# Attention scores in a hybrid encoder block: queries and keys kept as a high and a low part, heads taken one after the other

## The reference

```
for i in range(S // Q_BLOCK):                      # 4 query blocks of 128
    lo, hi = i * Q_BLOCK, (i + 1) * Q_BLOCK
    s = einsum('bhqd,bhkd->bhqk', qh[:, :, lo:hi], kh[:, :, :hi]) * scale
    s = s + cum_f[:, :, lo:hi, None] - cum_f[:, :, None, :hi]
    p = softmax(where(causal, s, -inf), axis=-1)
    outs.append(einsum('bhqk,bhkd->bhqd', p, vh[:, :, :hi]))
```

## Time and profile before

| | |
|---|---|
| median of three runs | 1771.42 us (1770.65 to 1771.48) |
| the profiled execution | 1769.05 us, span 1767.5 us |
| PE busy | 1723.1 us (97%) |
| DVE busy | 1343.8 us (76%) |
| ACT busy | 1108.6 us (63%) |
| attention steps q = 0 to 15 | from 260.6 us on, to the last transposes at 398.8 us |

### The profile page before, as it was taken

The page is one execution under the profiler, slowest core; times in us unless marked ns, Lnnn a source line. Parts: engine busy times, 40 slices in busy tenths (PEclk is TensorE's granted clock), DMA queues, the critical chain, the costliest instruction groups (busy, mean ns, idle before and its releaser), DMA issues.

```text
span 1767.5 us, 23399 instructions
## 1 busy us (share of the span) xinstructions
PE 1723.1 (97%) x8257; PEld 1403.7 (79%) x8258; DVE 1343.8 (76%) x1175; ACT 1108.6 (63%) x935; POOL 283.6 (16%) x227
## 2 busy tenths in 40 slices
PE   6999999999999999999999999999999999999995
PEld 5777788888887777888878888888888888888884
DVE  6334323442446898999999999999999999999998
ACT  3534434473322467777777777777777777777775
POOL 3000000000001162221212122212121212122211
PEclk9999999999999999999999999999999999999998
DMA  7432231212242599999999999999999999999994
GB/s 263 121 96 72 72 96 48 72 49 96 95 143 84 196 344 396 363 374 381 388 376 373 370 383 372 369 373 387 373 372 377 387 364 372 387 387 360 369 381 164
DMA packets 115696, 487.98 MB, mean 276 GB/s; under 512 B 18911, under 2 KB 49631, under 8 KB 66496
## 3 DMA queue, kind: packets, MB, share of 16 engines
q1 hardware_dynamic: 99576, 455.76, 67.0%
q0 software_dynamic: 16064, 31.55, 6.4%
q10 hardware_dynamic: 8, 0.01, 0.0%
HBM read 476.22 MB, written 28.36 MB: 285 GB/s over the span
## 4 chain that ended last, share of the span: by engine, by line
PE 90%; DVE 4%; ACT 2%; issue 2%; DMA 2%; ACTq 0%; POOLq 0%; DVEq 0%; SPq 0%
PE psA L1635 21%; PE psA L1637 21%; PE psA L1636 21%; PE psX L1637 6%; PE psX L1635 6%; PE psX L1636 6%; PE psX L1642 3%; DVE wlo L1382 2%; DMA raw<-in_w_down 1%; PE psX L1816 1%; ACT whi L961 1%; PE psX L1802 1%; PE psA L2011 1%; PE psX L1825 0%; PE psA L1891 0%
## 5 line engine op out<-in xcount | busy, mean ns | idle before, releaser
L1382 DVE TENSOR_TENSOR wlo<-raw,whi 128x2048 fp32r<-128x2048 f32 x382 | 863.2, 2287 | 63.7 <-ACT whi L961 62.5
L961 ACT CAST whi<-raw 128x2048 fp32r<-128x2048 f32 x382 | 724.7, 1913 | 199.6 <-PE psA L1637 170.1
L1635 PE MATMUL psA<-whi,xT_hi 128*128 128x512 f32 x1036 | 407.4, 393 | 2.2 <-issue 2.2
L1637 PE MATMUL psA<-whi,xT_lo 128*128 128x512 f32 x1036 | 404.0, 390 | 0.0
L1636 PE MATMUL psA<-wlo,xT_hi 128*128 128x512 f32 x1036 | 403.9, 390 | 0.0
L1635 PEld LDWEIGHTS psA<-whi,xT_hi 128*128 128x128 f32 x1036 | 195.0, 188 | 43.5 <-issue 4.2
L1637 PEld LDWEIGHTS psA<-whi,xT_lo 128*128 128x128 f32 x1036 | 194.8, 188 | 40.9
L1636 PEld LDWEIGHTS psA<-wlo,xT_hi 128*128 128x128 f32 x1036 | 194.9, 188 | 39.2
L1635 PE MATMUL psX<-whi,aT_hi 128*128 128x512 f32 x496 | 195.8, 395 | 0.0
L1637 PE MATMUL psX<-whi,aT_lo 128*128 128x512 f32 x496 | 193.4, 390 | 0.0
L1636 PE MATMUL psX<-wlo,aT_hi 128*128 128x512 f32 x496 | 193.3, 390 | 0.0
(11 more groups left out here) (371 smaller groups left out, 1998.4 us busy)
## 6 DMA issues: line engine op xcount, KB each, us to landing
raw<-in_w_gate_up SPq DMA_DIRECT2D x254, 1024.0 KB, 8.8
raw<-in_w_down SPq DMA_DIRECT2D x128, 1024.0 KB, 8.2
raw<-in_w_in SPq DMA_DIRECT2D x32, 1024.0 KB, 5.4
raw<-in_w_gla_proj SPq DMA_DIRECT2D x4, 1024.0 KB, 5.0
raw<-in_w_fox_proj SPq DMA_DIRECT2D x4, 1024.0 KB, 5.1
raw<-in_w_out SPq DMA_DIRECT2D x4, 1024.0 KB, 5.0
xt<-in_x SPq DMA_DIRECT2D x4, 512.0 KB, 6.0
h_dram<-xt POOLq DMA_DIRECT2D x4, 512.0 KB, 4.2
```

Source lines behind the costliest of these rows:

```text
L961: s_.copy(xsplit(c)[0], xraw(slot)).then_inc(hi_ready, 1)
L1382: v.tensor_tensor(lo, xraw(slot), hi.bitcast(F32), ALU.subtract).then_inc(lo_ready, 1)
L1635: mm(dst, sh, mh, start=first, stop=False)
L1637: return mm(dst, sl, mh, start=False, stop=last)
```

## The change

Queries and keys are kept in high and low parts, and the score product is made in three float32r passes in place of one float32 product.

- ACT writes the high part: queries into `q_of[i % 3][:, 0, :]` (head i, three buffers), keys into `k_of[i % 2][:, 0, :]` (two buffers). DVE writes the low part of each half, reading PSUM again, after its softmax of the same slot, and increments `qk_lo`.
- A step's two tiles are now of one head: step q = 2h has query blocks 0 and 3 of head h (128 and 512 columns), step 2h + 1 blocks 1 and 2 (256 and 384). So an odd step always has 256 and then 384 columns.
- A buffer may be written again when its last reader is done. ACT waits for this on `at_score` ahead of the copy of an odd head: queries of head i >= 3 wait for 4 (i - 2) finished tiles, keys of head i >= 2 for 4 (i - 1). With two tiles a step, these are the counts that step q = 1, 3, 5, 7, 9 or 11 reaches with its own second tile, in the very slot in which ACT makes the copy.
- PE waits for `qk_lo` ahead of each even step, and ahead of a chunk that writes a PSUM bank whose contents DVE still has to read.
- Four semaphores of the constant fills are one now, with the same order of fills and the same points waited for.

```
-        pair, q = divmod(s, TT)
-        return [(2 * pair, q), (2 * pair + 1, TT - 1 - q)]
+        h, part = divmod(s, 2)
+        return [(h, part), (h, TT - 1 - part)]
...
+        return 4 * (h // 2) + h % 2 + 3
...
                 elif kind == "fq":
-                    ins = s_.activation(fqk[j % 2][:, 0, half, :], src, ACT.Copy, scale=float(FHD) ** -0.5)
+                    if i % 2 == 1 and i >= 3:
+                        act.wait_ge(at_score, 4 * (i - 2))
+                    ins = s_.activation(q_of[i % 3][:, 0, :], src, ACT.Copy, scale=float(FHD) ** -0.5)
                 elif kind == "fk":
-                    ins = s_.copy(fqk[j % 2][:, 1, half, :], src)
+                    if i % 2 == 1 and i >= 2:
+                        act.wait_ge(at_score, 4 * (i - 1))
+                    ins = s_.copy(k_of[i % 2][:, 0, :], src)
...
+            c, half = divmod(s, 2)
+            if DENSE[c][0] in ("fq", "fk"):
+                i = 2 * DENSE[c][1] + half
+                dve.wait_ge(act_half, 2 * c + half + 1)
+                src = psA[:, 2 * (c % 2) + half, :]
+                if DENSE[c][0] == "fq":
+                    tile = q_of[i % 3]
+                    ins = v.scalar_tensor_tensor(tile[:, 1, :], src, float(FHD) ** -0.5, tile[:, 0, :].bitcast(F32),
+                                                 ALU.mult, ALU.subtract)
+                else:
+                    tile = k_of[i % 2]
+                    ins = v.tensor_tensor(tile[:, 1, :], src, tile[:, 0, :].bitcast(F32), ALU.subtract)
+                ins.then_inc(qk_lo, 1)
...
+                    if DENSE[c - 2][0] in ("fq", "fk"):
+                        pe.wait_ge(qk_lo, 2 * (c - 2 - FQ0) + 2)
...
-                if q % 4 == 0:
-                    pe.wait_ge(act_half, 2 * (18 + 2 * (q // 4)))
+                if q % 2 == 0:
+                    pe.wait_ge(qk_lo, split_qk(q // 2))
...
-                    mm(psX[:, b, 0:n], qk[:, 0, h % 2, t * P:(t + 1) * P], qk[:, 1, h % 2, 0:n], start=True, stop=False)
+                    mm(psX[:, b, 0:n], qh[:, 0, tok], kh[:, 0, 0:n], start=True, stop=False)
+                    mm(psX[:, b, 0:n], qh[:, 0, tok], kh[:, 1, 0:n], start=False, stop=False)
+                    mm(psX[:, b, 0:n], qh[:, 1, tok], kh[:, 0, 0:n], start=False, stop=False)
```

More of the change, by code:

```diff
@@ L77 @@
 WIDE = BY_TOKEN + ("wo",)
+FQ0 = 16
 GLA0 = 16
@@ L136, in build @@
     gq = at("gq", 136, [P, GH, T])
-    fqk = [at(f"fqk{b}", 112 + 8 * b, [P, 2, 2, T]) for b in range(2)]
+    q_of = [at(f"q_of{b}", kb, [P, 2, T], F32R) for b, kb in enumerate((116, 120, 112))]
+    k_of = [at(f"k_of{b}", kb, [P, 2, T], F32R) for b, kb in enumerate((138, 124))]
     probs = at("probs", 128, [P, 2, T])
@@ L295, in build @@
     const_ready = S("const_ready")
-    w_up_zero, eps_ready = S("w_up_zero"), S("eps_ready")
     x_in = [S(f"x_in{t}") for t in range(TT)]
     lnin_in, small_in, params_in, bias_in = S("lnin_in"), S("small_in"), S("params_in"), S("bias_in")
-    ones_ready, lnin_spread, lnin_ready = S("ones_ready"), S("lnin_spread"), S("lnin_ready")
+    first_fills, lnin_spread, lnin_ready = S("first_fills"), S("lnin_spread"), S("lnin_ready")
     lnmix_in, lnffn_in = S("lnmix_in"), S("lnffn_in")
@@ L339, in build @@
         S("stage_done"), S("stage_ready"), S("ridx_ready"), S("bias_added"))
+    qk_lo = S("qk_lo")
     fox_hi, fox_lo = S("fox_hi"), S("fox_lo")
@@ L421, in attention_tiles, with split_qk @@
     def attention_tiles(s):
-        pair, q = divmod(s, TT)
-        return [(2 * pair, q), (2 * pair + 1, TT - 1 - q)]
+        h, part = divmod(s, 2)
+        return [(h, part), (h, TT - 1 - part)]
+    def split_qk(h):
+        return 4 * (h // 2) + h % 2 + 3
     def chunk_state(n):
@@ L451, in load_params @@
             sp.dma_start(sm_raw[:, :, RANK:RANK + FH], w_in[:, :, C_FF:C_FF + FH]).then_inc(small_in, 16)
-            sp.wait_ge(w_up_zero, 1)
+            sp.wait_ge(first_fills, 4)
             for r in range(TT):
@@ L556, in _ @@
         g = nc.gpsimd
[L557 to L560, removed]
+        g.memset(ones[:], 1.0).then_inc(first_fills, 1)
+        g.memset(eps_c, EPS).then_inc(first_fills, 1)
+        g.memset(eps_f, EPS / ALPHA ** 2).then_inc(first_fills, 1)
+        g.memset(w_up[:], 0.0).then_inc(first_fills, 1)
         marks = Steps(pool, const_ready, 0)
@@ L787, in final_stats @@
             s_.activation(rstd[:, t:t + 1], asq[:, t:t + 1], ACT.Sqrt, bias=eps_f, scale=1.0 / D).then_inc(std_ready, 1)
-        act.wait_ge(eps_ready, 2)
+        act.wait_ge(first_fills, 3)
         s_.activation(warm, eps_c, ACT.Sqrt)
@@ L1644, in turn @@
             ins.then_inc(done, 1)
-        pe.wait_ge(ones_ready, 1)
+        pe.wait_ge(first_fills, 1)
         pe.wait_ge(lnin_in, 32)
@@ L1814, in hook @@
                         pe.wait_ge(at_max, 2 * (q - 1) + b + 1)
-                    qk = fqk[(h // 2) % 2]
-                    mm(psX[:, b, 0:n], qk[:, 0, h % 2, t * P:(t + 1) * P], qk[:, 1, h % 2, 0:n], start=True, stop=False)
+                    qh, kh = q_of[h % 3], k_of[h % 2]
+                    tok = slice(t * P, (t + 1) * P)
+                    mm(psX[:, b, 0:n], qh[:, 0, tok], kh[:, 0, 0:n], start=True, stop=False)
+                    mm(psX[:, b, 0:n], qh[:, 0, tok], kh[:, 1, 0:n], start=False, stop=False)
+                    mm(psX[:, b, 0:n], qh[:, 1, tok], kh[:, 0, 0:n], start=False, stop=False)
                     mm(psX[:, b, 0:n], sel[:, h * P:(h + 1) * P], fneg[:, 0:n], start=False, stop=False)
```

## The result

The changed kernel takes 1774.51 us (median of 17 runs, 1772.08 to 1778.95), the kernel before 1770.94 us beside it (17 runs, 1769.10 to 1772.09). The ratio is 1.0023, with a 95% interval from 1.0016 to 1.0031: slower by 3.6 us as the medians stand, 2.8 to 5.5 us by the interval. Forecast were 3.0 us, and 1774.4 us for the median. It lies on the line between what I called no difference that can be told and slower.

A forecast was written before the change was run, and what follows sets the result against it. PE was taken to bound the kernel, busy for 149.64 of 150 us in the attention. Terms: -2.8 (passes) + 5.8 (ACT's wait) - 0.15 (last wait) = +2.9, with picking up +3.0 us: 1771.42 to 1774.4 us, range 1771.2 to 1778.0.

The forecast's parts named there:

- no difference that can be told: Whole kernel: median between 1767.9 and 1775.0 us, about 0.2% (3.5 us) being what the measurement can tell; chance 0.56.
- PE is the bound and a shift arrives at the end: Attention and experts: PE runs almost without a gap, so a shift in the attention reaches the end one to one.
- The wait of ACT: Odd steps 3 to 11: ACT's wait for at_score delays foxT copies and PE's transposes, 5 x 1.16 = 5.8 us lost.
- The gain of the passes: PE's scores: three float32r passes for float32 gain 0.26 us an odd step, 0.09 an even one, 2.8 us in all.
- the model: PE's scores: columns / 2.4 GHz plus 0.014 us an instruction, float32 at four times the columns; 1.55 us against 1.57 read.
- The low parts on DVE are covered: DVE in the attention: 16 low parts of 0.69 us, 11 us in all, fit idle times of 1.83 us.
- The order of heads and the last wait: Behind the last scores (wait 0.36 us): step 15's new tile widths let the chain begin sooner, 0.15 us gained.
- The loads of the added products are hidden: PE's scores: weight loads of 32 added instructions overlap running products; unhidden they would lose 3.5 us.
- The rival of unhidden loads: PE's short passes: weight loads not hidden, own work a loss of 0.7 us, stalls stay, 1777.9 us; chance 0.10.
- the rival of short passes at 0.067 us: PE's 128-column products as fast as their columns: gain 4.2 us with the stalls, 1773.0 us; chance 0.12.
- scores longer than 1.57 us in even steps: Sign of being wrong, in PE's even steps; the prediction expected 1.48 us there and 1.31 in odd steps.
- The chance of 0.38 for slower: Whole kernel: median above 1775.0 us, summed as 0.10 (loads) + 0.06 (DVE) + 0.22 (a third of the likeliest case).

The follow-up runs named there:

- e6: e1 with only the high x high product of queries and keys, the two passes with low parts left out: 1758.99 us, ratio 0.9933 to the kernel before.
- e2: The kernel before plus only ACT's wait for the slot's own score tiles in odd slots 37 to 47: 1775.92 us, ratio 1.0030 to the kernel before.
- e5: e1 with each of DVE's 16 low parts of queries and keys made twice: 1769.17 us, ratio 0.9994 to the kernel before.
- e7: The kernel before with only the new order of tiles, in float32 and without new waits: 1770.53 us, ratio 1.0002 to the kernel before.
- e1: The changed kernel with ACT's two foxT copies ahead of its query or key copy in odd slots 39 to 47: 1768.32 us, ratio 0.9988 to the kernel before.
- e3: The changed kernel with four query and three key high-part buffers, so ACT's waits ask for an earlier step's tiles: 1768.61 us, ratio 0.9987 to the kernel before.
- e4: e1 with both masks of a step side by side behind the two tiles' other products: 1767.26 us, ratio 0.9983 to the kernel before.
- e8: e4 with the foxT copies first in slots 38 to 53, also where ACT fills the gates: 1768.32 us, ratio 0.9986 to the kernel before.

## Why the prediction was right

- *PE is the bound and a shift arrives at the end.* From step 3 on +4.4 us (125.25 - 120.88). The gain of steps 0 to 2 lies ahead of that: counted from the first score product, at 260.59 us before and 260.84 in the changed kernel, the whole attention is 409.22 - 260.84 = 148.38 us against 404.86 - 260.59 = 144.27, +4.1 us. At the end it is +3.6 us (2.8 to 5.5); e6 and e2 give, by the medians, 9.3 for 10.5 and 5.4 for 6.0. The runs fit one to one within their intervals.
- *The wait of ACT.* Right in place, number and way: steps 3, 5, 7, 9 and 11, through the `foxT` copies queued behind it. Size forecast 1.16 us each; measured 9.74 - 8.51 = 1.23, so 6.15 us in place of 5.8. Of the difference of 0.07 us 0.05 us is the pick-up by ACT: from the mask's end at 286.62 to 286.71, 0.09 us, where I took 0.04 from a row that waited for `half_done`.
- *The gain of the passes.* Right in sign, too large: forecast 0.26 and 0.09 us a step, 2.8 us; measured 0.20 (8.71 - 8.51) and 0.045 (8.705 - 8.66), 2.0 us. e6 tells which term was off. If the pass that e6 keeps costs as much as the two that it leaves out, three passes cost 3 x 0.30 = 0.90 us in an odd step and 3 x 0.355 = 1.065 in an even one, so the float32 product had cost 1.10 and 1.11, close to the 1.12 of the model (4 x 640 / 2400 + 4 x 0.014). The passes had been charged at 0.295 and 0.337. The rest is that I subtracted a modelled new step from a read old one, and the model was 0.02 us short of the reading in every step. Modelled against modelled would have taken 0.3 us off the gain.
- *The low parts on DVE are covered.* Shown by e5, even at twice their number. No wait of PE for `qk_lo` is listed, and DVE's maxima wait for PE alone.
- *The order of heads and the last wait.* The new order is free (e7). In the changed kernel the last step is 409.22 - 401.67 = 7.55 us against 7.70: the 0.15 forecast. But e7, with the order alone, has 7.67, so the order was the wrong reason for most of it, and that the size came out is luck. Where DVE makes the maxima of step 15, the traces show a difference that nobody counted on:

```profile
392.04 0.48 DVE L1239 TENSOR_SCALAR_CACHE_REDUCE probs<-psX,small 128x256 f32<-128x256 f32 x1 [5.56 <-PE psX L1825]
393.05 0.62 DVE L1239 TENSOR_SCALAR_CACHE_REDUCE probs<-psX,small 128x384 f32<-128x384 f32 x1 [0.33 <-issue]
396.08 0.48 DVE L1249 TENSOR_SCALAR_CACHE_REDUCE probs<-psX,small 128x256 f32<-128x256 f32 x1 [5.01 <-PE psX L1853]
396.73 0.62 DVE L1249 TENSOR_SCALAR_CACHE_REDUCE probs<-psX,small 128x384 f32<-128x384 f32 x1
```

The first two lines are e7, the last two the changed kernel. The second maximum starts 1.01 us behind the first in e7 and 0.65 in the changed kernel. The idle 0.33 us ("issue": no wait that the profile shows) stands in the same place in the kernel before (393.06) and in e2, and not in e1, e3, e4, e5, e6 and e8, nor in e7's other odd steps (374.62 to 375.27, 0.65 us). So, counted from the outputs of step 15, ACT's chain began some 0.36 us sooner by this, and 0.20 by the shorter scores. Why the gap is there stays open, and what each of the two is worth at the last step was not tried.
- *The loads of the added products are hidden.* The rival of unhidden loads would have made three passes dearer than the float32 product; e1 is faster than before, so it falls. So does the rival of short passes at 0.067 us: they start 0.11 to 0.12 apart. That their weight loads set this distance fits the 0.11 us between loads and is argued, not shown.
- *One sign was badly chosen.* The prediction named scores longer than 1.57 us in even steps as a sign of being wrong. Read as it read the kernel before, from the first score product to the transposes, step 2 has 277.95 - 276.34 = 1.61 us, and step 3, with its transposes due at 286.46, has 1.46 in place of the 1.31 named. But the first score product now starts 1.03 us behind the outputs (283.97 to 285.00), not 1.12, so part of the time has only changed its place. Outputs and scores together take 277.95 - 275.31 = 2.64 us in step 2, against 295.37 - 292.68 = 2.69 before, and 286.46 - 283.97 = 2.49 in step 3, against 338.90 - 336.21 = 2.69: shorter in both.

The two errors, 0.8 us too much gain and 0.35 too little stall, both made the forecast too low: 3.0 + 0.8 + 0.35 = 4.15 us, against the 4.1 measured over the whole attention. The timed difference of 3.6 us lies between, and the median came out within 0.1 us of the forecast because the kernel before, too, came out lower, 1770.94 in place of 1771.42 us; that is luck. The chance of 0.38 for slower was somewhat low: with the terms as measured the median would be 1771.42 + 4.1 = 1775.5 us, above the line of 1775.0, and slower was the likelier side.

## What to carry to other kernels

A wait added to an engine's stream can cost through what stands behind the waiting instruction though nobody is waiting for that instruction itself: look at the next few instructions of that engine and at who waits for them. When a reused buffer's wait names work of the same slot, either move the instructions that others need ahead of it or add a buffer; here both gave the same 6 us. And where a gain and a stall of similar size meet, compute both old and new from the same model, since the 0.02 us between model and reading in each of 16 steps was a tenth of the answer.

## What the runs showed of the hardware

- A float32 product of 128 x 128 by n columns costs PE about four times its columns at 2.4 GHz: 1.10 us for 640 columns, whose columns take 0.267 us (by e1 and e6, if the three passes cost alike). A float32r pass costs 0.30 us for tiles of 256 and 384 columns, but 0.355 for 128 and 512: at 128 columns the 0.11 to 0.12 us between starts is the same as at 256.
- A bf16 mask of 128 columns between float32r products costs more than its columns (0.053 us at 2.4 GHz): from the first mask of step 2 to the second product behind it are 277.18 - 276.83 = 0.35 us, of which that product's own distance is 0.23, and moving the mask away saved 0.03 to 0.07 us a step (e4).
- Five idle times of PE of about 1 us, 18.4 us apart, left the granted clock at 1.00 from 250 to 400 us.
